# Eight query projections around an attention of eight head couples: two of them placed whole, or three of them in halves, on one Trainium2 core

## The chip, the cores and the metric

The kernel runs on one core of a Trainium2 chip (trn2). Five instruction streams are written out by hand and meet at semaphores: TensorE (PE in the profile, its weight loads PEld), VectorE (DVE), ScalarE (ACT), GpSimd (POOL) and SyncE (SP), which issues nearly all of the transfers. The metric is the device time of one execution in microseconds.

## The reference

A two-layer network on 256 tokens of 1024 features. Layer one is a short convolution mixer and a gated feed-forward block. Layer two is an attention block followed by a second feed-forward block. Cut to the part in question:

```python
kv = nsa_shared_kv(rmsnorm(x, kv_norm), w_kv, cmp_pe, cmp_w1, cmp_b1, cmp_w2)
qg = h @ w_qg                          # h is [256, 1024]: 16 heads x 64 of queries, 48 gate columns
# per head: compressed, selected and windowed branch
o_c = softmax(q @ k_cmp + bias_c) @ v_cmp       # 15 compressed blocks
o_s = softmax(q @ k_slc + bias_s) @ v_slc       # 256 keys, causal
o_w = softmax(q @ k_win + bias_w) @ v_win       # 256 keys, causal
o = g[..., 0:1] * o_c + g[..., 1:2] * o_s + g[..., 2:3] * o_w
x = x + o @ w_o
```

`k_cmp` and `v_cmp` come from a small gelu network over blocks of 32 tokens: `gelu(blk @ cmp_w1 + cmp_b1) @ cmp_w2`.

## The kernel before

**Pieces.** All large weights come in pieces of 128x1024 f32 (512 KB). A float32 product is made of three matmuls on two fp32r parts of each operand, so each piece is treated three times before TensorE uses it: SP loads it into `staged`, ScalarE casts it into `w_hi` (function `lead`, L529), and VectorE subtracts the two and writes the remainder to `w_lo` (function `rest`, L746). Six such remainders are given to GpSimd instead (L438). Pieces rotate through six slots; the load of a piece waits for the remainder of the piece six places earlier, the cast of a piece for TensorE's use of that earlier piece. The counters `hi_up`, `lo_up` and `used_up` rise by one for each piece in order, so one engine's remainders and another's must follow each other in piece order.

**Order.** `B_ORDER` lists the pieces of the attention block: 12 for keys and values, four `w1` (the first product of the compressing network), the gate, eight `q` (one for each couple of heads, a 128x128x8 product of 24 matmuls of 256 columns, L1090 to L1092), and eight of the output projection (`o`). TensorE, VectorE and ScalarE walk this list up to `("q", Q_BEFORE - 1)`, here `("q", 4)`. At each entry `b` ScalarE casts piece b + 6 and VectorE makes its remainder, so that the walk covers the pieces up to the third `o` piece.

**Compressed keys and values.** When all four `w1` products are in, VectorE computes a tanh gelu (L938 to L961, then L964 and L966 behind a ScalarE tanh, L684); TensorE's `compressed()` (L1266, L1269) waits for it (`hidden_done`) and stands behind `q` 3; VectorE copies its result out (L972, L975).

**Attention.** Heads go in couples: `scores(i)` (L1344 to L1350), then per head an exponential on ScalarE (L696), `weigh` on VectorE (L1023 to L1034, the far spans) and GpSimd (L486, the near spans), `turn` on TensorE (transposes, L1362 to L1373), copies out of PSUM (`keep_turned`, L1043 and L1045 on VectorE, L708 on ScalarE) and `attend` (L1387 to L1394). VectorE's `bias_and_maximum` (L991, L994, L1013) is what the next but one couple's exponentials wait for. On TensorE couple `i` is the stretch `turn(2i)`, `turn(2i + 1)`, `scores(i + 2)`, `attend(i)`. `q` 5 stands between `scores(0)` and `scores(1)`; `q` 6 and `q` 7 stand whole between the two turns of couples 0 and 5 (`Q_CYCLE = {0: 6, 5: 7}`). After couple 5 the output projection (`project`) is woven into the last two couples.

**What follows a query.** Each query product is copied out by VectorE (`query`, L912), and `scores(i)` waits for the copy of query max(i, 2). Queries 3 to 7 share one PSUM bank.

Of the kernel before, what the change touches and what calls it, by code (L numbers as in the profile page):

```python
# [50 lines left out]
for _name, _n in (("gains", 6 * KT), ("a_taps", 3 * AU), ("f_taps", 2 * 2 * FU * 3), ("pe", 2 * 16),  # L51
# [5 lines left out]


B_ORDER = ([("cmp", t) for t in range(4)] + [("key", t) for t in range(4)] + [("val", t) for t in range(4)]
           + [("w1", 0), ("gate", 0), ("w1", 1), ("q", 0), ("w1", 2), ("q", 1), ("w1", 3)] + [("q", t) for t in range(2, 8)]  # L60
           + [("o", t) for t in range(8)])
NB = len(B_ORDER)
UP_SLOTS, DOWN_SLOTS = 6, 3
# [2 lines left out]
KEEP_WARM = 5  # L66
O_FIRST = B_ORDER.index(("o", 0))

Q_BEFORE = 5
Q_RING = 6  # L70


# [1 line left out]
def q_index(t):  # L74
    return B_ORDER.index(("q", t))
# [50 lines left out]
def build(nc, xT, xt, par, final, hot, rel, a_up, a_down, f_up, f_down, b_up, b_down, scratch, out):  # L126
    piece = plan_pieces()
    ctx = ExitStack()
    with ctx:
# [284 lines left out]
        @block.gpsimd  # L414
        def _(pool):
            nc.gpsimd.memset(ones[:], 1.0).then_inc(consts_done, 1)
            nc.gpsimd.memset(ident[:], 0.0).then_inc(consts_done, 1)
            nc.gpsimd.memset(eps[:], EPS).then_inc(consts_done, 1)
            nc.gpsimd.memset(rowmask[:], 1.0).then_inc(consts_done, 1)
            pool.wait_ge(consts_done, 4)  # L420
            nc.gpsimd.affine_select(out=ident[:], in_=ident[:], compare_op=ALU.not_equal, fill=1.0, base=0,
                                    pattern=[[-1, P]], channel_multiplier=1).then_inc(consts_done, 1)


            nc.gpsimd.affine_select(out=rowmask[:], in_=rowmask[:], compare_op=ALU.is_ge, fill=0.0, base=P - CL,
                                    pattern=[[0, 1]], channel_multiplier=-1).then_inc(consts_done, 1)
            nc.gpsimd.memset(vc[:], 0.0).then_inc(consts_done, 1)

            def pads(n):
                nc.gpsimd.memset(shifted[:, :, :, 0:2], 0.0).then_inc(padded, 1)  # L430

            def rest(st, kind, k, c):

                q = piece_of(st, kind, k, c)
                hi, lo = (hi_up, lo_up) if kind == "up" else (hi_down, lo_down)
                pool.wait_ge(hi, q["n"] + 1)
                pool.wait_ge(lo, q["n"])
                nc.gpsimd.tensor_tensor(w_lo[:, q["slot"], :], staged[:, min(q["slot"], UP_SLOTS), :],  # L438
                                        w_hi[:, q["slot"], :].bitcast(F32), ALU.subtract).then_inc(lo, 1)

            pads(0)


            pool.wait_ge(rows_copied, 1)
            pool.dma_start(scratch, rows_sb).then_inc(rows_stored, 16)
            pool.wait_ge(rows_stored, 16)
            diagonals = bass.AP(tensor=scratch.tensor, offset=0, ap=[[1, P], [384, HEADS], [1, T]])
            pool.dma_start(bias[:], diagonals).then_inc(bias_landed, 16)
            nc.gpsimd.memset(ends_bias[:], NEG).then_inc(ends_ready, 1)
            pool.wait_ge(ends_ready, 1)  # L450
            pool.wait_ge(bias_landed, 16)
            nc.gpsimd.tensor_copy(ends_bias[:, :, 0, 0:NC0], bias[:, :, P + CL - 1::CS]).then_inc(ends_ready, 1)
            nc.gpsimd.tensor_copy(ends_bias[:, :, 1, :], bias[:, :, CL - 1::CS]).then_inc(ends_ready, 1)
            rest("a", "down", AU - 1, 0)
            rest("f0", "up", 1, 1)
            rest("f0", "down", FU - 1, 0)
            rest("b", "up", 3, 0)
            for j in range(2):

                pool.wait_ge(tokens_shifted, j + 1)  # L460
                if j:

                    pool.wait_ge(block_lo_done, 1)
                tok, pe_j = tokens[:, j, 0, 0:1], params[:, PAR["pe"] + 16 * j:PAR["pe"] + 16 * j + 16]
                tok = bass.AP(tensor=tok.tensor, offset=tok.offset, ap=[tok.ap[0], [2, 16], [T, GROUPS], [CS, NC]])
                pe_j = pe_j.unsqueeze(2).unsqueeze(3).to_broadcast([P, 16, GROUPS, NC])
                nc.gpsimd.tensor_tensor(block_in.rearrange("p (i g c) -> p i g c", i=16, g=GROUPS), tok, pe_j,
                                        ALU.add).then_inc(block_done, 1)
                pool.wait_ge(block_hi_done, j + 1)
                nc.gpsimd.tensor_tensor(blocks[j][:, 1, :], block_in, blocks[j][:, 0, :].bitcast(F32),  # L470
                                        ALU.subtract).then_inc(block_lo_done, 1)

            pool.wait_ge(block_lo_done, 2)
            for r in range(2):
                nc.gpsimd.memset(ends_soft[:, r, :, :, NC:32], 0.0).then_inc(zeroed, 1)
            def lower_ends(i):

                pool.wait_ge(ends_maxed, i + 1)
                nc.gpsimd.tensor_tensor(ends_of(i), ends_of(i), over_ends(ends_max[:, i % 2]), ALU.subtract).then_inc(ends_lowered, 1)

            lower_ends(0)
            for e in range(HEADS):

                pool.wait_ge(weighted, e + 1)
                for n in NEAR:
                    q = nc.gpsimd.tensor_scalar(span(e, n), span(e, n), stats_of(e, 12 + n, 13 + n), None, ALU.mult)  # L486
                q.then_inc(normed, 1)
                if e % 2:
                    nc.gpsimd.tensor_tensor(ends_of(e // 2), ends_of(e // 2), over_ends(stats[:, e // 2 % 2, :, 12:14]),
                                            ALU.mult).then_inc(ends_weighted, 1)  # L490
                elif e + 2 < HEADS:
                    lower_ends(e // 2 + 1)

            pool.wait_ge(headed, HEADS // 2)
            pads(1)
            rest("f1", "up", 1, 1)
            rest("f1", "down", FU - 1, 0)
# [236 lines left out]
        def _(dve):  # L734
# [180 lines left out]
            for b, (what, t) in enumerate(B_ORDER):  # L915
# [50 lines left out]
                    nc.vector.tensor_tensor(hid, th, z, ALU.mult).then_inc(hidden_done, 1)  # L966
                if what == "q":
                    query(t)
                if (what, t) == ("q", 3):
                    dve.wait_ge(cmp_mm, 1)  # L970
                    for p in range(2):
                        nc.vector.tensor_copy(keysT[HD * p:HD * p + HD, :, 0:NC],  # L972
                                              bank[6][0:HD, 128:128 + 60].rearrange("p (a q c) -> p a q c", a=2, q=2)[:, :, p, :])
                    for p in range(2):
                        q = nc.vector.tensor_copy(vc[32 * p:32 * p + NC, :, HD * p:HD * p + HD],  # L975
                                                  bank[6][32 * p:32 * p + NC, 256:512].rearrange("p (a q c) -> p a q c", a=2, q=2)[:, :, p, :])
                    q.then_inc(cmp_done, 1)
                rest("b", "up", b + AHEAD, 0)
                if (what, t) == ("q", Q_BEFORE - 1):
                    break  # L980
            dve.wait_ge(bias_landed, 16)
            dve.wait_ge(ends_ready, 3)
            dve.wait_ge(zeroed, 2)
# [70 lines left out]

            bias_and_maximum(0)
            bias_and_maximum(1)
            query(5)
            for i in range(HEADS // 2 - 1):
                weigh(2 * i)
                bias_and_maximum(2 * i + 2)  # L1060
                weigh(2 * i + 1)
                keep_turned(2 * i)
                bias_and_maximum(2 * i + 3)
                if i >= 1:
                    rest_heads(i - 1)
                if i in Q_CYCLE:
                    query(Q_CYCLE[i])
                keep_turned(2 * i + 1)
            weigh(HEADS - 2)
            rest("b", "up", q_index(5) + AHEAD, 0)  # L1070
# [16 lines left out]
        def _(pe):  # L1087
# [164 lines left out]
            def queries(t):  # L1252
                if t == 3:

                    pe.wait_ge(gate_done, 1)
                elif t > 3:

                    pe.wait_ge(b_evacuated, 8 + t)
                product(piece_of("b", "up", q_index(t), 0), q_bank(t), gq_hi, gq_lo, True)

            def compressed():

                pe.wait_ge(hidden_done, 1)
# [12 lines left out]
            for b in range(4, q_index(Q_BEFORE - 1) + 1):  # L1276
# [9 lines left out]
                if what == "q":  # L1286
# [4 lines left out]
                    if t == 0:  # L1291
# [3 lines left out]
                            mm = nc.tensor.transpose(bank[7][:, T + 3 * HEADS * k:T + 3 * HEADS * (k + 1)],  # L1295
                                                     gateT[:, k * P:k * P + P], ident[0:3 * HEADS, 0:3 * HEADS])
                        mm.then_inc(gate_turned, 1)
                    if t == 3:
                        compressed()
                    continue  # L1300
                pe.wait_ge(lo_up, q["n"] + 1)
# [105 lines left out]
            pe.wait_ge(cmp_done, 1)  # L1407
            pe.wait_ge(vals_done, 2)
            scores(0)
            queries(5)  # L1410
            scores(1)
            for i in range(HEADS // 2 - 2):
                turn(2 * i)
                if i in Q_CYCLE:
                    queries(Q_CYCLE[i])
                turn(2 * i + 1)
                scores(i + 2)
                attend(i)
# [15 lines left out]


SPANS = [None, None, (0, P), (P, T), (P + T, P), (2 * P + T, T)]
Q_CYCLE = {0: 6, 5: 7}
LEAD_AFTER = {3: 5, 5: 6, 11: 7}
NEAR, FAR = (2, 4), (3, 5)


def head_of(e):
# [10 lines left out]
NOTHING = ([], [], [])  # L1453


AFTER_POOL = {("f0", "down", 0, 0), ("f0", "up", 2, 0), ("b", "up", 4, 0), ("f1", "down", 0, 0), ("f1", "up", 2, 0)}


def UPS(st, k, i=0):
# [73 lines left out]
```

## Time and profile before

| | before |
|---|---|
| median of 3 runs | 632.47 us (631.91 to 633.13) |
| the profiled execution, whole | 633.22 us |
| span in the profile | 631.5 us |
| granted TensorE clock, mean | 0.994 |
| PE / PEld busy | 97% / 85% |
| DVE / ACT / POOL busy | 77% / 62% / 9% |
| projections of the attention block | about 295 to 355 us |
| attention of eight couples | about 355 to 423 us |

The profiled execution spends 633.22 - 631.5 = 1.7 us outside the span. A timeline row gives the start, the time from start to end of a run of like instructions, the engine, line, operation and shapes, and in square brackets how long the engine sat idle before it and what released it. Matmuls overlap, so the time that one takes of TensorE is the distance from its start to the start of the next, not its own duration. The same holds by some 0.1 us for VectorE and ScalarE.

### The profile page before, as it was taken

The numbers are of one execution on the slowest core, as the hardware profiler recorded it, in microseconds if no ns is written. First come the engines' busy times: TensorE is split into PE (matmuls) and PEld (weight loads), VectorE is DVE, ScalarE is ACT, GpSimd is POOL, SyncE is SP. The second block draws the span as 40 slices with busy tenths as digits, with TensorE's granted clock in tenths as the row PEclk, the third lists the DMA queues.
The fourth block names the chain that finished last, engine by engine and source line by source line (L and its number), as shares of the span: only waits on it lengthen the run. The fifth ranks groups of instructions, "written<-read, shape, count | busy, mean of one in ns | idle before, by whom it ended". The sixth has DMA issues, their size and how long they took to land.

```text
span 631.5 us, 11277 instructions
## 1 busy us (share of the span) xinstructions
PE 610.9 (97%) x3738; PEld 534.1 (85%) x3738; DVE 485.1 (77%) x939; ACT 388.6 (62%) x708; POOL 59.4 (9%) x78
## 2 busy tenths in 40 slices
PE   7999999999999999999999898998999999999995
PEld 7999997888888888888989776777888888888884
DVE  4787756788888777777878789847788888777865
ACT  6644445666666666668556478717766666666644
POOL 0110002000000000011131144421000000000010
PEclk8999999999999999999999999999999999999998
DMA  8797432465656555761476400033365555555531
GB/s 310 290 336 241 179 133 100 166 203 194 205 201 202 199 189 179 287 241 34 146 245 214 142 2 2 1 101 133 118 206 193 209 201 207 192 178 195 199 101 66
DMA packets 30640, 109.55 MB, mean 173 GB/s; under 512 B 3419, under 2 KB 3691, under 8 KB 30476
## 3 DMA queue, kind: packets, MB, share of 16 engines
q1 hardware_dynamic: 30044, 106.97, 48.6%
q0 software_dynamic: 560, 2.12, 0.9%
q8 instruction: 20, 0.33, 0.2%
q14 instruction: 16, 0.13, 0.1%
HBM read 108.00 MB, written 1.07 MB: 173 GB/s over the span
## 4 chain that ended last, share of the span: by engine, by line
PE 88%; DVE 5%; ACT 3%; issue 2%; POOL 1%; DMA 1%; SPq 0%; DVEq 0%; ACTq 0%
PE bank L1129 24%; PE bank L1090 15%; PE bank L1091 15%; PE bank L1092 15%; PE bank L1133 13%; POOL work L486 1%; PE bank L1109 1%; DVE work L1013 1%; PE bank L1362 1%; DMA staged<-in_a_up 1%; ACT work L533 1%; PE bank L1320 1%; PE bank L1150 1%; PE bank L1110 1%; ACT w_hi L529 1%
## 5 line engine op out<-in xcount | busy, mean ns | idle before, releaser
L746 DVE TENSOR_TENSOR w_lo<-staged,w_hi 128x1024 fp32r<-128x1024 f32 x191 | 236.6, 1247 | 41.9 <-ACT w_hi L529 41.9
L529 ACT ACTIVATE w_hi<-staged 128x1024 fp32r<-128x1024 f32 x197 | 199.8, 1046 | 26.6 <-PE bank L1092 15.7
L1129 PE MATMUL bank<-gx,w_hi 128*128 128x512 f32 x672 | 167.2, 391 | 0.0
L1129 PEld LDWEIGHTS bank<-gx,w_hi 128*128 128x128 f32 x672 | 123.2, 188 | 23.8
L1133 PEld LDWEIGHTS bank<-gx,w_lo 128*128 128x128 f32 x672 | 91.7, 190 | 6.6
L1133 PE MATMUL bank<-gx,w_lo 128*128 128x256 f32 x672 | 93.7, 282 | 0.0
L1090 PE MATMUL bank<-w_hi,y 128*128 128x512 f32 x208 | 81.5, 392 | 0.0
L1091 PE MATMUL bank<-w_lo,y 128*128 128x512 f32 x208 | 81.5, 392 | 0.0
L1092 PE MATMUL bank<-w_hi,y 128*128 128x512 f32 x208 | 80.9, 389 | 0.0
L615 ACT ACTIVATE work<-work,params 128x256 f32<-128x256 f32 x96 | 44.2, 504 | 57.4 <-DVE work L847 39.2
L1090 PE MATMUL bank<-gx,w_hi 128*128 128x256 f32 x256 | 73.4, 287 | 2.6 <-DVE w_lo L746 2.1
L1091 PE MATMUL bank<-gx,w_hi 128*128 128x256 f32 x256 | 73.1, 285 | 0.0
L1092 PE MATMUL bank<-gx,w_lo 128*128 128x256 f32 x256 | 73.0, 285 | 0.0
L629 ACT ACTIVATE y<-work 128x256 fp32r<-128x256 f32 x52 | 21.7, 418 | 77.8 <-DVE work L868 59.8
L438 POOL TENSOR_TENSOR w_lo<-staged,w_hi 128x1024 fp32r<-128x1024 f32 x6 | 14.5, 2415 | 424.9 <-ACT w_hi L529 424.9
L1090 PEld LDWEIGHTS bank<-gx,w_hi 128*128 128x128 f32 x256 | 49.8, 195 | 3.8 <-DVE w_lo L746 3.0
L1091 PEld LDWEIGHTS bank<-gx,w_hi 128*128 128x128 f32 x256 | 49.8, 194 | 0.2
L1092 PEld LDWEIGHTS bank<-gx,w_lo 128*128 128x128 f32 x256 | 49.8, 194 | 0.0
L847 DVE TENSOR_TENSOR work<-bank,work 128x512 f32<-128x512 f32 x44 | 30.4, 691 | 24.6 <-ACT work L611 24.5
L1092 PEld LDWEIGHTS bank<-w_hi,y 128*128 128x128 f32 x208 | 39.1, 188 | 8.5
L1090 PEld LDWEIGHTS bank<-w_hi,y 128*128 128x128 f32 x208 | 39.2, 189 | 7.1
L854 DVE SCALAR_TENSOR_TENSOR work<-work,params 128x256 f32<-128x256 f32 x96 | 42.4, 479 | 3.6 <-ACT work L615 3.5
(160 smaller groups left out, 818.7 us busy)
## 6 DMA issues: line engine op xcount, KB each, us to landing
staged<-in_f_up SPq DMA_DIRECT2D x88, 512.0 KB, 5.2
staged<-in_f_down SPq DMA_DIRECT2D x44, 512.0 KB, 3.3
staged<-in_a_up SPq DMA_DIRECT2D x24, 512.0 KB, 7.3
staged<-in_b_up SPq DMA_DIRECT2D x24, 512.0 KB, 4.3
staged<-in_a_down SPq DMA_DIRECT2D x8, 512.0 KB, 3.5
staged<-in_b_down SPq DMA_DIRECT2D x8, 512.0 KB, 4.2
bias<-bias_rows POOLq DMA_DIRECT2D x1, 2048.0 KB, 11.5
bias<-in_xT SPq DMA_DIRECT2D x4, 256.0 KB, 5.2
```

Source lines behind the costliest of these rows:

```text
L438: nc.gpsimd.tensor_tensor(w_lo[:, q["slot"], :], staged[:, min(q["slot"], UP_SLOTS), :], w_hi[:, q["slot"], :].bitcast(F32), ALU.subtract) ...
L529: nc.scalar.activation(w_hi[:, q["slot"], 0:n], staged[:, s, 0:n], ACT.Copy).then_inc(hi, 1)
L615: nc.scalar.activation(conv[:, r, c, :], shifted[:, r, c, 2:2 + T], ACT.Copy, scale=tap(st, c, i, k, 2)).then_inc(tapped[st], 1)
L629: nc.scalar.activation(y_hi[:, r * T:(r + 1) * T], conv[:, r, 1, :], ACT.Copy).then_inc(y_hi_done[st], 1)
L746: nc.vector.tensor_tensor(w_lo[:, q["slot"], 0:n], staged[:, s, 0:n], w_hi[:, q["slot"], 0:n].bitcast(F32), ALU.subtract).then_inc(lo, 1)
L847: nc.vector.tensor_tensor(shifted[:, r, :, 2:2 + T], pair_of(st, k, 0), shifted[:, r, :, 2:2 + T], ALU.add).then_inc(scaled[st], 1)
L854: nc.vector.scalar_tensor_tensor(conv[:, r, c, :], shifted[:, r, c, 1:1 + T], tap(st, c, i, k, 1), conv[:, r, c, :], ALU.mult, ALU.add).th ...
L1090: nc.tensor.matmul(out_ap, whi, xhi, start=start, stop=False, skip_group_check=True)
L1091: nc.tensor.matmul(out_ap, whi, xlo, start=False, stop=False, skip_group_check=True)
L1092: return nc.tensor.matmul(out_ap, wlo, xhi, start=False, stop=stop, skip_group_check=True)
L1129: nc.tensor.matmul(dst, w_hi[:, s, kt * P:kt * P + P], gx[:, kt, :], start=kt == 0, stop=False, skip_group_check=True)
L1133: mm = nc.tensor.matmul(dst[:, 0:T], w_lo[:, s, kt * P:kt * P + P], gx_hi[:, kt, :], start=False, stop=kt == KT - 1, skip_group_check=True)
```

## The change

Query 4 leaves the walk ahead of attention and takes the place of query 5 between the first two scores. Queries 5, 6 and 7 are cut into two halves of 12 matmuls each, and the six halves stand one in each of couples 0 to 5, between the two turns. To let `compressed()` come one query earlier, the last `w1` piece is put ahead of `q` 1, and `compressed()` stands behind `q` 2. The walk on ScalarE and VectorE ends one entry earlier, and VectorE's walk no longer makes the remainders of the second and third `o` piece: GpSimd makes them in half tiles behind heads 5, 7, 9 and 11. ScalarE's casts of the later `o` pieces stand behind heads 1, 3, 7 and 11 (before: 3, 5 and 11).

```diff
-           + [("w1", 0), ("gate", 0), ("w1", 1), ("q", 0), ("w1", 2), ("q", 1), ("w1", 3)] + [("q", t) for t in range(2, 8)]
+           + [("w1", 0), ("gate", 0), ("w1", 1), ("q", 0), ("w1", 2), ("w1", 3), ("q", 1)] + [("q", t) for t in range(2, 8)]
...
-Q_BEFORE = 5
+Q_BEFORE = 4
...
+            def rest_half(b, h):
+
+                q = piece_of("b", "up", b, 0)
+                cols = slice(h * 512, h * 512 + 512)
+                if h == 0:
+                    pool.wait_ge(hi_up, q["n"] + 1)
+                    pool.wait_ge(lo_up, q["n"])
+                r = nc.gpsimd.tensor_tensor(w_lo[:, q["slot"], cols], staged[:, q["slot"], cols],
+                                            w_hi[:, q["slot"], cols].bitcast(F32), ALU.subtract)
+                if h:
+                    r.then_inc(lo_up, 1)
...
                 elif e + 2 < HEADS:
                     lower_ends(e // 2 + 1)
+                if e in REST_AFTER:
+                    rest_half(*REST_AFTER[e])
...
-                if (what, t) == ("q", 3):
+                if (what, t) == ("q", 2):
                     dve.wait_ge(cmp_mm, 1)
...
-                rest("b", "up", b + AHEAD, 0)
                 if (what, t) == ("q", Q_BEFORE - 1):
                     break
+                rest("b", "up", b + AHEAD, 0)
...
-            query(5)
+            query(4)
...
-                if i in Q_CYCLE:
-                    query(Q_CYCLE[i])
+                if i % 2 and i < 6:
+                    query(Q_HALVES + i // 2)
                 keep_turned(2 * i + 1)
...
+            def half_queries(t, n):
+
+                q = piece_of("b", "up", q_index(t), 0)
+                s = q["slot"]
+                if n == 0:
+                    pe.wait_ge(b_evacuated, 8 + t)
+                    pe.wait_ge(lo_up, q["n"] + 1)
+                for kt in range(4 * n, 4 * n + 4):
+                    mm = three(q_bank(t), w_hi[:, s, kt * P:kt * P + P], w_lo[:, s, kt * P:kt * P + P], gq_hi[:, kt, :], gq_lo[:, kt, :],
+                               kt == 0, kt == KT - 1)
+                if n:
+                    mm.then_inc(used_up, 1)
...
-                    if t == 3:
+                    if t == 2:
                         compressed()
...
-            queries(5)
+            queries(4)
             scores(1)
             for i in range(HEADS // 2 - 2):
                 turn(2 * i)
-                if i in Q_CYCLE:
-                    queries(Q_CYCLE[i])
+                half_queries(Q_HALVES + i // 2, i % 2)
                 turn(2 * i + 1)
...
-Q_CYCLE = {0: 6, 5: 7}
-LEAD_AFTER = {3: 5, 5: 6, 11: 7}
+Q_HALVES = 5
+LEAD_AFTER = {1: 4, 3: 5, 7: 6, 11: 7}
 NEAR, FAR = (2, 4), (3, 5)
+REST_AFTER = {5: (q_index(Q_BEFORE - 1) + AHEAD, 0), 7: (q_index(Q_BEFORE - 1) + AHEAD, 1),
+              9: (q_index(Q_BEFORE) + AHEAD, 0), 11: (q_index(Q_BEFORE) + AHEAD, 1)}
```

In addition the fourth `o` piece's remainder on VectorE waits for the count that GpSimd's last half gives (`AFTER_POOL`).

## Rows read from the trace of the kernel before

**Rows 1.** The page's busy times by engine, over the whole span.
```profile
PE 610.9 (97%) x3738; PEld 534.1 (85%) x3738; DVE 485.1 (77%) x939; ACT 388.6 (62%) x708; POOL 59.4 (9%) x78
```

**Rows 2.** TensorE's waits, 338 to 412 us: in total, times, longest.
```profile
PE bank L1362 <- POOL work L486: 6.3, 6, 1.4
PE bank L1344 <- DVE stats L1013: 0.5, 1, 0.5
```

**Rows 3.** Windows: length, then busy time per engine, granted clock, DMA share, GB/s.
```profile
371.30:377.80 6.50, 5.51 (x49) 3.90 (x48) 6.16 (x34) 6.04 (x21) 3.29 (x6) 1.00 0.00 1
397.40:405.60 8.20, 8.20 (x74) 6.81 (x73) 6.62 (x35) 6.17 (x21) 3.30 (x6) 1.00 0.01 2
```

**Rows 4.** Timeline of TensorE, couple 0, which holds query 6.
```profile
363.13 0.66 PE L1362 MATMUL bank<-ident,work 128*128 128x128 f32 x4 [1.37 <-POOL work L486]
...
363.76 0.36 PE L1090 MATMUL bank<-gq_hi,w_hi 128*128 128x256 f32 x1
363.96 0.28 PE L1091 MATMUL bank<-gq_lo,w_hi 128*128 128x256 f32 x1
...
366.71 0.60 PE L1362 MATMUL bank<-ident,work 128*128 128x128 f32 x4
...
367.68 0.51 PE L1344 MATMUL bank<-work 64*128 64x143 f32 x4
```

**Rows 5.** Timeline of TensorE, couple 1, which holds no query, and the next turn.
```profile
371.31 0.66 PE L1362 MATMUL bank<-ident,work 128*128 128x128 f32 x4
...
373.18 0.66 PE L1362 MATMUL bank<-ident,work 128*128 128x128 f32 x4 [0.99 <-POOL work L486]
...
374.20 0.52 PE L1344 MATMUL bank<-work 64*128 64x143 f32 x4
...
377.83 0.66 PE L1362 MATMUL bank<-ident,work 128*128 128x128 f32 x4
```

**Rows 6.** Timeline of VectorE, one couple from copy to copy, and the copy of query 7.
```profile
374.31 0.42 DVE L1043 COPY work<-bank 128x256 f32<-128x256 f32 x1
...
377.99 0.17 DVE L1030 TENSOR_TENSOR stats<-stats,gate 128x6 f32<-128x6 f32 x1
...
380.29 0.41 DVE L1051 TENSOR_TENSOR gx<-bank,gx 128x256 fp32r<-128x256 f32 x1
380.83 0.42 DVE L1043 COPY work<-bank 128x256 f32<-128x256 f32 x1
...
381.96 0.17 DVE L1030 TENSOR_TENSOR stats<-stats,gate 128x6 f32<-128x6 f32 x1
...
401.18 0.42 DVE L912 TENSOR_SCALAR work<-bank 128x256 f32<-128x256 f32 x1 [0.92 <-PE bank L1092]
```

**Rows 7.** Timeline of GpSimd, head 1 in couple 0, then the couple of rows 6.
```profile
365.60 0.29 POOL L489 TENSOR_TENSOR work<-work,stats 128x60 f32<-128x60 f32 x1
...
378.26 1.39 POOL L486 TENSOR_SCALAR work<-work,stats 128x128 f32<-128x128 f32 x2 [0.91 <-DVE stats L1030]
379.62 0.29 POOL L489 TENSOR_TENSOR work<-work,stats 128x60 f32<-128x60 f32 x1
382.23 1.39 POOL L486 TENSOR_SCALAR work<-work,stats 128x128 f32<-128x128 f32 x2 [2.32 <-DVE stats L1030]
```

**Rows 8.** Timeline of TensorE from the compressed product to the second scores.
```profile
351.26 0.33 PE L1266 MATMUL bank<-work,params 128*64 128x60 f32 x2
...
351.85 0.39 PE L1090 MATMUL bank<-gq_hi,w_hi 128*128 128x256 f32 x1
...
354.90 0.52 PE L1344 MATMUL bank<-work 64*128 64x143 f32 x4
...
356.46 0.38 PE L1090 MATMUL bank<-gq_hi,w_hi 128*128 128x256 f32 x1
...
360.13 0.52 PE L1344 MATMUL bank<-work 64*128 64x143 f32 x4 [0.54 <-DVE stats L1013]
```

**Rows 9.** Timeline of VectorE at the start of attention.
```profile
356.16 1.23 DVE L746 TENSOR_TENSOR w_lo<-staged,w_hi 128x1024 fp32r<-128x1024 f32 x1 [0.72 <-ACT w_hi L529]
357.30 0.21 DVE L991 TENSOR_TENSOR work<-bank,ends_bias 128x60 f32<-128x60 f32 x1
...
359.90 0.42 DVE L912 TENSOR_SCALAR work<-bank 128x256 f32<-128x256 f32 x1
```

**Rows 10.** Timeline of VectorE ahead of the compressed product.
```profile
344.38 0.42 DVE L912 TENSOR_SCALAR work<-bank 128x256 f32<-128x256 f32 x1
344.97 1.23 DVE L746 TENSOR_TENSOR w_lo<-staged,w_hi 128x1024 fp32r<-128x1024 f32 x1 [0.17 <-ACT w_hi L529]
...
348.84 0.29 DVE L966 TENSOR_TENSOR work<-work 128x120 f32<-128x120 f32 x1
```

**Rows 11.** GpSimd's whole remainder (line view: ns min/median/max), and two-input work of GpSimd and VectorE together.
```profile
L438 POOL TENSOR_TENSOR w_lo<-staged,w_hi x6: 2384/2408/2483, 93.4 to 614.0; 128x1024 fp32r<-128x1024 f32 x6
...
332.61 2.39 POOL L470 TENSOR_TENSOR gx<-work,gx 128x960 fp32r<-128x960 f32 x1 [8.53 <-ACT gx L674]
...
333.51 2.57 DVE L746 TENSOR_TENSOR w_lo<-staged,w_hi 128x1024 fp32r<-128x1024 f32 x1 [0.62 <-ACT w_hi L529]
```

**Rows 12.** The page's group of ScalarE's casts: busy, mean ns; idle before.
```profile
L529 ACT ACTIVATE w_hi<-staged 128x1024 fp32r<-128x1024 f32 x197 | 199.8, 1046 | 26.6 <-PE bank L1092 15.7
```

More of the change, by code:

```diff
@@ L1453 @@
 NOTHING = ([], [], [])
-AFTER_POOL = {("f0", "down", 0, 0), ("f0", "up", 2, 0), ("b", "up", 4, 0), ("f1", "down", 0, 0), ("f1", "up", 2, 0)}
+AFTER_POOL = {("b", "up", q_index(Q_BEFORE + 1) + AHEAD, 0), ("f0", "down", 0, 0), ("f0", "up", 2, 0), ("b", "up", 4, 0), ("f1", "down", 0, 0), ("f1", "up", 2, 0)}
 def UPS(st, k, i=0):
```

## The prediction

> **What bounds the kernel now.** I read the page first: TensorE is busy 97% of the span, VectorE 77% [rows 1]. TensorE's work is the same before and after, matmul for matmul, so the change can only win time in which TensorE stands still, and it can lose only where it makes new standstill. The second view is therefore the list of TensorE's waits over the stretch that the change touches: 6 waits for GpSimd's L486, 6.3 us in all, and one of 0.5 us for VectorE's L1013 [rows 2]. The third view, the windows by couple, shows the pattern: a couple without a query lasts 6.5 us with TensorE busy for 5.5, a couple with a whole query 8.2 us with TensorE never idle; the granted clock is 1.00 in both, the upper of its two levels (2.4 GHz) [rows 3]. Last the timelines, for the chain that sets the 6.5 us.
>
> That chain is a cycle. Let K be the start of VectorE's copy of the odd head's turn, 374.31. Its L1030 is at K + 3.7, GpSimd's L486 starts at K + 3.95 and is through at 379.62 = K + 5.3, the next odd turn starts 0.1 later, takes about 1 us, and the next copy is at 380.83 = K + 6.52 [rows 6, 7]. VectorE is itself nearly full: its last step L1051 starts at 380.29 and gives way about 0.34 later, at K + 6.3 [rows 6]. TensorE, for its part, goes from one even turn to the next in 6.52 us, from 371.31 to 377.83, and waits 0.99 of it [rows 5]; with query 6 it takes 371.31 - 363.13 = 8.18 [rows 4, 5]. The query costs 366.71 - 363.76 = 2.95 us of TensorE [rows 4] but lengthens the couple by only 1.66: a couple has room for 1.29 us of other work. Couples 0 and 5 hold 2.95 each and use the room up; couples 1 to 4 leave it empty.
>
> **Step 1: query 4 leaves the stretch ahead of attention.** The stretch from `compressed()` to the first scores is 354.90 - 351.26 = 3.64 [rows 8] and keeps its make-up. What moves is the whole of it, one query earlier. A query there is worth 2.96 (from 351.85 to 354.90 less 0.09 of signal) [rows 8]. TensorE would be at `compressed()` at 351.26 - 2.96 = 348.30. But `compressed()` needs VectorE's L966, and that is not one query earlier. Before, it ends at 348.84 + 0.29 = 349.13, 2.1 us ahead of its use [rows 8, 10]. Between 343 and 349 VectorE has its queue full: the same remainders, the copy of query 1 and the gelu in another order, with one gap, from the end of L912's share (344.38 + 0.33) to 344.97, 0.26 us [rows 10]. The earlier `w1` piece lets only that gap go. So L966 ends at about 348.87, with the signal 349.0, and TensorE stands still for 0.7 us. A new wait; it eats a quarter of this step. The first scores start 351.26 - 349.0 = 2.26 earlier, at 352.64.
>
> **Step 2: one remainder less in front of the first maximum.** Before, the first scores are out at about 356.5 but VectorE makes the third `o` piece's remainder until 357.30, and only then starts L991 [rows 8, 9]. Without L746 it starts 0.1 to 0.15 after the scores, 1.71 after their start, at 354.35: 2.95 earlier than 357.30. The second scores wait for L1013 as before (359.90 to 360.13 [rows 8, 9]); query 4 in the place of query 5 ends at 352.64 + 1.56 + 2.98 = 357.2, L1013 at 356.95 with the signal 357.2, so that this wait of 0.5 us goes, but turn 0 hangs on VectorE, ScalarE and GpSimd, not on the scores. It comes 2.95 earlier, at 360.18 instead of 363.13 [rows 4]. **Gain of steps 1 and 2: 2.95 us.**
>
> **Step 3: halves in six couples.** In the whole query the first matmul takes 363.96 - 363.76 = 0.20 and the other 23 take 2.75 / 23 = 0.12 each [rows 4]. A half is 0.20 + 11 x 0.12 = 1.52. A couple in which TensorE never waits then takes 8.18 - 2.95 + 1.52 = 6.75. Is the cycle quick enough? TensorE comes to the next odd turn 0.97 (turn, 366.71 to 367.68 [rows 4]) + 3.63 (scores and attend, 374.20 to 377.83 [rows 5]) + 0.63 (even turn, 363.13 to 363.76 [rows 4]) + 1.52 = 6.75 after the last, which is K + 5.67; GpSimd is through at K + 5.3, plus 0.1. It holds by 0.28. In couple 0 the pipeline is not yet in step: GpSimd releases turn 1 at 365.60 = 2.47 after turn 0 [rows 4, 7], with the signal 2.55, TensorE is there after 0.63 + 1.52 = 2.15. That leaves 0.40, and 0.05 for a turn that starts cold: 7.20. Six couples took 2 x 8.18 + 4 x 6.52 = 42.44 and take 7.20 + 5 x 6.75 = 40.95. **Gain 1.49 us.** The seventh couple has the same chain at its odd turn and stays.
>
> **Step 4: copies of queries 5 to 7.** They lie on VectorE in couples 1, 3 and 5, between L1051 and the next copy. VectorE reaches that place at K + 6.32, the copy adds 0.34, and 6.66 is still below 6.75. But `scores(7)` waits for the copy of query 7: written at K + 6.32 + 0.42 = 6.74 [rows 6], signalled at 6.81, wanted at 6.75 - 0.11 = 6.64. **Loss 0.15 us.** The copies of 5 and 6 are wanted two couples later and cost nothing.
>
> **Step 5: half tiles on GpSimd.** A whole remainder is 2.41 us there [rows 11], 60 columns are 0.29 [rows 7]; on the line through both 512 columns are 1.3 (bounds: half of 2.41, 1.2, and 1.6 if it is crowded as VectorE's is in rows 11 by a third). Behind an odd head GpSimd is free from 379.62 + 0.29 = 379.91 to 382.23 [rows 7], 2.3 us. The half ends at 381.2. The first VectorE instruction after it that reads two SBUF operands is L1030 at 381.96 [rows 6]; until then VectorE works on PSUM operands. So the cover is 0.75 us towards VectorE and 1.0 towards L486: cost nothing. If the cover were gone, VectorE would stand as in rows 11, where L746 takes 2.57 instead of 1.23 beside a GpSimd L470 that began 0.9 earlier. That row speaks against the change in general.
>
> The Trainium skill says why, in "SBUF — State Buffer", section "Who interferes with whom": a VectorE instruction with two SBUF inputs and a GpSimd one that reads SBUF exclude each other for a whole instruction, the first to issue wins. The trace agrees with the 2.57. Applied to the place of the halves the rule gives the same zero; should they slip by 0.75 it gives the slower rival below.
>
> **Step 6: casts.** ScalarE's four casts (1.05 each [rows 12]) stand behind odd heads, where it waits for attend's end anyway. They wait for TensorE's use of queries 4 to 7, which in each case lies ahead of the turn that the cast stands behind. The `o` pieces are first wanted after couple 6. Nothing, and at most 0.3 each if an exponential is held up. The load of the last `o` piece hangs on GpSimd's second half and comes some 30 us later than before, still 20 us ahead of need; the second layer's feed-forward loads hang on VectorE's remainders behind head 14, which keep their distance from the end of attention.
>
> **Sum:** 2.95 + 1.49 - 0.15 = 4.29 us. Against the profiled execution: span 631.5 - 4.3 = 627.2, whole 633.22 - 4.29 = 628.9. That execution was 0.75 above the median; from the median 632.47 it is 628.2.
>
> **Rivals.** *More is gained:* VectorE reaches L966 in time, the wait of step 1 is small. For it: VectorE's order is new and a copy may wait less. Against it: from 343.25 to 349.13 only 0.26 us are free. Without the wait 627.5. *The handovers cost more, because VectorE sets the odd couples:* 6.66 against 6.75 leaves no room; if each of couples 1, 3 and 5 takes VectorE's 6.66 plus the 0.2 us by which its queue stood empty before the copy at 380.83 [rows 6], if the even couples don't win it back, and if the halves cost 1.6 instead of 1.52, then 3 x 0.11 + 6 x 0.08 and a wait of `compressed()` longer by half a remainder (0.6) give 628.2 + 1.4 = 629.6. *It does not do what it says:* the couples keep their standstill and the half comes on top, 6.52 + 1.52 = 8.04 in each of six couples, 48.2 instead of 42.4; with step 1 and 2 that is 632.47 - 2.95 + 5.8 = 635.3. This decides if the odd head's chain started only behind the half. The code has no such wait, and couple 0 shows a query filling 1.29 of standstill. *Slower by the shared port:* the half is still running when L1030 and the far spans' L1034 want SBUF, or holds up L486. Point from which it decides: a half later or longer by 0.75. Price by rows 11: 2.57 - 1.23 = 1.35 on VectorE's part of the cycle, four times 5.4, less the 0.3 of slack in one couple, and as much again, 1.1, for L486 pushed behind it: 628.2 + 6.2 = 634.4. *No difference:* parts of both last cases in one or two couples, or a later stage that gives the time back; I see none, since everything after couple 6 hangs on the attention itself.
>
> **How the numbers follow.** A measurement of this kernel tells 0.2%, 1.3 us, from no change. Forecast 0.66 (its own range 627.4 to 629.2), more gained 0.10, handovers 0.13, no difference 0.06, the two slower ones 0.05 together. The range takes in the first three with the spread of three runs, 0.6: 626.8 to 630.3. Faster by over 0.2% (below 631.2): 0.89; within: 0.07; slower: 0.04.
>
> **What would show it.** TensorE's waits: L1362 for L486 down to about two or three (turn 0, turn 1, turn 13), the 0.5 for L1013 gone, a new one of 0.7 on L1266 for L966. First scores at 352.6, turn 0 at 360.2, even turns 6.75 apart, turn 12 at 401.1 (before 405.58). GpSimd has four remainders of 128x512 of 1.2 to 1.3 us each, and VectorE's L1030 keeps its 0.17 behind them. The prediction is wrong if a couple takes over 7 us, if L966 ends before 348.3, or if turn 13 and later stand still more than before.

## The result

The changed kernel takes 628.51 us (median of 4 runs, 627.70 to 628.83) against 632.25 us for the kernel before: ratio 0.9928, 95% interval 0.9915 to 0.9941, so 0.7% faster (the two medians by themselves give 628.51 / 632.25 = 0.9941). The forecast was 628.2 in a range of 626.8 to 630.3. Two later rounds of the same kernel gave 0.9923 (0.9906 to 0.9939) and 0.9943 (0.9926 to 0.9960). In the last of them four of six runs had a low granted clock, which the forecast knew nothing of; that is taken up below.

The page of the changed kernel, its busy times:

```profile
span 627.1 us, 11282 instructions
PE 610.6 (97%) x3738; PEld 534.4 (85%) x3738; DVE 482.8 (77%) x937; ACT 388.2 (62%) x708; POOL 63.3 (10%) x82
```

TensorE's busy time is within 0.3 us of that in [rows 1], the span is 4.4 us shorter. TensorE's waits between 338 and 412 us (total, times, longest), which answer to [rows 2]:

```profile
PE bank L1389 <- POOL work L498: 2.5, 3, 1.4
PE bank L1293 <- DVE work L980: 0.4, 1, 0.4
```

The six waits for GpSimd (6.3 us) are three (2.5), the 0.5 for L1013 is gone, and a new one stands in front of the compressed product. The timeline of TensorE from that product to the first turn, which answers to [rows 8] and the first of [rows 4]:

```profile
348.99 0.33 PE L1293 MATMUL bank<-work,params 128*64 128x60 f32 x2 [0.45 <-DVE work L980]
...
352.64 0.51 PE L1371 MATMUL bank<-work 64*128 64x143 f32 x4
...
357.25 0.52 PE L1371 MATMUL bank<-work 64*128 64x143 f32 x4
...
360.25 0.66 PE L1389 MATMUL bank<-ident,work 128*128 128x128 f32 x4 [1.37 <-POOL work L498]
```

And the same view for couples 1, 5 and 6, where [rows 5] stood:

```profile
367.46 0.66 PE L1389 MATMUL bank<-ident,work 128*128 128x128 f32 x4
...
369.60 0.60 PE L1389 MATMUL bank<-ident,work 128*128 128x128 f32 x4
...
374.20 0.66 PE L1389 MATMUL bank<-ident,work 128*128 128x128 f32 x4
...
394.44 0.66 PE L1389 MATMUL bank<-ident,work 128*128 128x128 f32 x4
...
396.59 0.60 PE L1389 MATMUL bank<-ident,work 128*128 128x128 f32 x4
...
397.69 0.52 PE L1371 MATMUL bank<-work 64*128 64x143 f32 x4
...
401.33 0.66 PE L1389 MATMUL bank<-ident,work 128*128 128x128 f32 x4
...
403.06 0.66 PE L1389 MATMUL bank<-ident,work 128*128 128x128 f32 x4 [0.86 <-POOL work L498]
```

Couple 1 takes 374.20 - 367.46 = 6.74 and TensorE goes into its odd turn without a wait. To compare executions that don't begin equally fast I use one anchor, the gate's transposes ahead of the third w1 piece (338.62 before, 338.70 after), and one end, the first projection matmul (408.29 before, 403.90 after). The four rows, first of the kernel before, then of the changed kernel:

```profile
338.62 0.32 PE L1295 MATMUL bank<-ident,work 48*128 48x48 f32 x2
...
408.29 0.48 PE L1090 MATMUL bank<-w_hi,gx 128*128 128x512 f32 x1
```

```profile
338.70 0.32 PE L1322 MATMUL bank<-ident,work 48*128 48x48 f32 x2
...
403.90 0.47 PE L1104 MATMUL bank<-w_hi,gx 128*128 128x512 f32 x1
```

That stretch is 69.67 before and 65.20 after: **4.47 us less**. Behind it both kernels take the same, 631.5 - 408.29 = 223.2 and 627.1 - 403.90 = 223.2. Everything gained is gained in this stretch and nothing of it is given back later.

### The profile page after: what moved, and what is told of

The parts are those of the page before. It is cut to its first block, busy times and chain, and to the rows that moved or that the text cites. A ratio compares the mean times of both kernels' runs of the same rounds, so it can differ in the third digit from the quotient of the medians.

```text
span 627.1 us, 11282 instructions
## 1 busy us (share of the span) xinstructions
PE 610.6 (97%) x3738; PEld 534.4 (85%) x3738; DVE 482.8 (77%) x937; ACT 388.2 (62%) x708; POOL 63.3 (10%) x82
## 4 chain that ended last, share of the span: by engine, by line
PE 88%; DVE 5%; ACT 3%; issue 1%; DMA 1%; POOL 0%; SPq 0%; DVEq 0%; ACTq 0%
PE bank L1143 24%; PE bank L1104 14%; PE bank L1105 14%; PE bank L1106 14%; PE bank L1147 13%; DVE w_lo L760 2%; PE bank L1123 1%; PE bank L1389 1%; ACT w_hi L543 1%; DMA staged<-in_a_up 1%; ACT work L547 1%; PE bank L1421 1%; PE bank L1164 1%; PE bank L1414 1%; PE bank L1124 1%
```

## The experiments

The first theory is the prediction's: the couple has room for a half but not for a whole query, and VectorE's queue sets the start of the compressed product. Rivals are that only the earlier start counts, that VectorE and GpSimd hold each other up and so take the gain, and that the remainders on GpSimd bring most of it.

### The changed kernel again

> The changed kernel itself, as the mark for its neighbours on the same chip. Expected: ratio to the kernel before 0.993, span 627.1 us, turn 12 some 41.1 us after turn 0.

Ratio 0.9923, span 627.8, 41.1 us from turn 0 to turn 12. But the compressed product stands 11.41 us behind the anchor instead of 10.29. The windows (length, then busy time and count of PE, PEld, DVE, ACT, POOL, granted clock, DMA share, GB/s) of this execution:

```profile
338.00:342.00 4.00, 4.00 (x36) 3.81 (x35) 3.96 (x7) 2.62 (x3) 0.00 (x0) 0.99 0.57 198
342.00:346.00 4.00, 4.00 (x23) 4.00 (x23) 3.79 (x10) 1.06 (x1) 0.00 (x0) 0.58 0.86 295
```

and of the execution profiled first:

```profile
342.00:346.00 4.00, 4.00 (x36) 4.00 (x36) 3.79 (x11) 1.38 (x3) 0.00 (x0) 1.00 0.87 267
```

In the one, TensorE's clock goes down to 0.50 (the lower level, 1.2 GHz) from 341.9 to 345.3 us; in the other it does not. This was not in my reckoning, and it is taken up again below. For the other experiments I therefore compare pieces of the timeline that lie clear of it.

### Halves without the earlier start

```diff
-                if i in Q_CYCLE:
-                    queries(Q_CYCLE[i])
+                if i < 4:
+                    half_queries(6 + i // 2, i % 2)
```

(in the kernel before; VectorE copies them out in couples 1 and 3)

> Query 4 stays ahead of attention, query 5 between the first two scores; only queries 6 and 7 are cut into halves, in couples 0 to 3. My theory (a couple has 1.29 us of standstill which a half of 1.52 fills): couples of 7.2, 6.75, 6.75, 6.75, 6.52, 6.52 us, 40.5 against 42.4 before, so 1.95 us faster than the kernel before, ratio 0.997. Rival (the half comes on top of the 6.52): four couples of 8.04, no gain, 45.2, ratio 1.004.

Ratio 0.9975 (0.9962 to 0.9987). The even turns of couples 3 to 5:

```profile
384.02 0.66 PE L1375 MATMUL bank<-ident,work 128*128 128x128 f32 x4
...
390.77 0.66 PE L1375 MATMUL bank<-ident,work 128*128 128x128 f32 x4
392.63 0.66 PE L1375 MATMUL bank<-ident,work 128*128 128x128 f32 x4 [0.99 <-POOL work L486]
...
397.29 0.66 PE L1375 MATMUL bank<-ident,work 128*128 128x128 f32 x4
```

Couple 3, with a half, takes 6.75; couple 4, without, 6.52 and its 0.99 of waiting. From anchor to first projection 67.73, against 69.67 before: 1.94 less where 1.95 was expected. The rival, a half on top of the 6.52, is out.

### Whole queries in three couples

```diff
-                half_queries(Q_HALVES + i // 2, i % 2)
+                if i % 2 == 0:
+                    queries(Q_HALVES + i // 2)
```

(VectorE copies them out in the same even couples)

> The changed kernel with queries 5, 6 and 7 whole in couples 0, 2 and 4 instead of in halves in couples 0 to 5. My theory: three couples of 8.18 and three of 6.52, 44.1 us from turn 0 to turn 12 against 41.1 with halves, so 3.0 us slower than the changed kernel (ratio to before about 0.998). Rival (the gain of the change lies in the earlier start alone and the halves do nothing): same as the changed kernel, 0.993.

Ratio 0.9983 (0.9970 to 0.9996). Turn 0 and turn 12:

```profile
361.54 0.66 PE L1389 MATMUL bank<-ident,work 128*128 128x128 f32 x4 [1.37 <-POOL work L498]
...
405.65 0.66 PE L1389 MATMUL bank<-ident,work 128*128 128x128 f32 x4
```

The couples take 8.18, 6.53, 8.18, 6.52, 8.18, 6.52, in all 44.11 us from turn 0 to turn 12 against 401.33 - 360.25 = 41.08 with halves: 3.03 more, 3.0 expected. Against the 405.58 - 363.13 = 42.45 of the kernel before, the loop with three whole queries is 1.7 us longer and eats more than half of the earlier start; with halves it is 1.4 shorter.

### The last w1 piece in its old place

```diff
-           + [... ("w1", 2), ("w1", 3), ("q", 1)] ...
+           + [... ("w1", 2), ("q", 1), ("w1", 3)] ...
```

> The changed kernel with the last w1 piece behind query 1 again; compressed() stays behind query 2. My theory (VectorE's queue, not the w1 product, sets the time of L980, and the order frees only one gap of 0.26 us): the compressed product starts 0.26 us later, the whole 0.3 us slower than the changed kernel. Rival (the product itself has to be early): the w1 product ends one query later, 2.9 us, and the compressed product with it, 2 to 3 us slower.

Ratio 0.9943 (0.9921 to 0.9964), five runs. The compressed product:

```profile
349.31 0.33 PE L1293 MATMUL bank<-work,params 128*64 128x60 f32 x2 [0.73 <-DVE work L980]
```

That is 349.31 - 338.74 = 10.57 behind the anchor, 0.28 more than with the piece moved (0.26 expected). The rival's 2 to 3 us are out. Moving the w1 product is worth a quarter of a microsecond, since VectorE's queue decides. That is little against what the neighbourhood of the two products goes with in other executions: the 1.1 us of `after_again`.

### The halves behind the even heads

```diff
-REST_AFTER = {5: ..., 7: ..., 9: ..., 11: ...}
+REST_AFTER = {4: ..., 6: ..., 8: ..., 10: ...}
```

> The changed kernel with the same four halves behind the even heads 4, 6, 8 and 10, where GpSimd is free for only 0.9 us. If VectorE's L1044 and GpSimd's half exclude each other for a whole instruction: VectorE's L1044 of the odd head stands 0.6 us, L498 starts 0.8 us late, of which 0.28 is slack: 0.5 us for each of four couples, 2 us slower than the changed kernel. If only GpSimd's own queue counts: L498 0.36 us late, 0.1 us for each, 0.4 us slower.

Ratio 0.9969 (0.9957 to 0.9981). GpSimd and VectorE in couple 3:

```profile
383.11 1.27 POOL L488 TENSOR_TENSOR w_lo<-staged,w_hi 128x512 fp32r<-128x512 f32 x1
384.50 1.39 POOL L498 TENSOR_SCALAR work<-work,stats 128x128 f32<-128x128 f32 x2
```

```profile
383.57 0.18 DVE L1041 RECIPROCAL stats<-stats 128x6 f32<-128x6 f32 x1
383.79 0.61 DVE L1044 TENSOR_TENSOR stats<-stats,gate 128x6 f32<-128x6 f32 x1
384.43 0.73 DVE L1048 TENSOR_SCALAR work<-work,stats 128x256 f32<-128x256 f32 x2
```

L1044, six columns from two SBUF operands, takes 0.61 instead of 0.17 and ends at 384.40, when the half ends (384.38). L1041, with one SBUF operand, ran at its usual speed beside the same half. The same 0.61 stands in all four couples that hold a half. So these two instructions exclude each other. The price is 1.2 us where I expected 2: the couples from 2 to 5 take 6.97, 6.97, 7.09 and 7.32, which is 0.23, 0.23, 0.33 and 0.43 over those of the changed kernel. L1044 met the half late and lost 0.44, not 0.6. Less the 0.28 of slack that L498 has, 0.16 a couple would be left; why the later couples lose more than the earlier ones is not worked out. The expectation was wrong in size; that L1044 stands until the half is through is shown.

### Whole remainders on GpSimd

```diff
-                if e in REST_AFTER:
-                    rest_half(*REST_AFTER[e])
+                if e in (7, 11):
+                    rest("b", "up", q_index(Q_BEFORE - 1 + (e == 11)) + AHEAD, 0)
```

> The changed kernel with the two remainders on GpSimd whole, behind heads 7 and 11, instead of in halves behind 5, 7, 9 and 11. My theory: a whole one runs 2.4 us from 383.0, ends 0.1 us after VectorE's L1044 wants to start and before L498 does, so each costs 0.1 to 0.2 us at VectorE and next to nothing at TensorE: within 0.3 us of the changed kernel. Rival (the port costs as L746 beside L470 did, 1.35 us each): 2.0 to 2.7 us slower.

Ratio 0.9938 (0.9920 to 0.9955).

```profile
382.97 2.37 POOL L438 TENSOR_TENSOR w_lo<-staged,w_hi 128x1024 fp32r<-128x1024 f32 x1
385.56 1.39 POOL L498 TENSOR_SCALAR work<-work,stats 128x128 f32<-128x128 f32 x2 [0.22 <-DVE stats L1044]
```

The whole piece ends at 385.34, and L1044 of the next head takes its usual 0.17 from 385.29, so the 0.1 to 0.2 us that I expected it to lose are not there. From anchor to first projection 65.22 against 65.20. Dividing the remainders into halves gains nothing here; a whole one just fits the same gap. The halves only leave a wider margin.

### The remainders on VectorE

```diff
+                rest("b", "up", b + AHEAD, 0)
                 if (what, t) == ("q", Q_BEFORE - 1):
                     break
-                rest("b", "up", b + AHEAD, 0)
```

(and the other one ahead of the fourth `o` piece's, behind head 14; none on GpSimd)

> The changed kernel with the two remainders back on VectorE, one at the end of the walk, ahead of the first maximum, one behind head 14's weights; GpSimd makes none in attention. My theory: the first remainder has to wait for its cast and ends at 355.0, the first maximum (354.4 in the changed kernel) starts 0.55 us later, and so does all behind it; the second costs nothing: 0.5 us slower. Rival (the remainders were worth a whole L746 each): 2.4 us slower.

Ratio 0.9950 (0.9935 to 0.9965).

```profile
356.98 1.23 DVE L758 TENSOR_TENSOR w_lo<-staged,w_hi 128x1024 fp32r<-128x1024 f32 x1 [0.72 <-ACT w_hi L541]
358.13 0.21 DVE L1003 TENSOR_TENSOR work<-bank,ends_bias 128x60 f32<-128x60 f32 x1
```

```profile
355.73 0.51 PE L1370 MATMUL bank<-work 64*128 64x143 f32 x4
...
363.95 0.66 PE L1388 MATMUL bank<-ident,work 128*128 128x128 f32 x4 [1.38 <-POOL work L498]
```

The first scores start at 355.73 and turn 0 at 363.95, 8.22 later, against 360.25 - 352.64 = 7.61 in the changed kernel: 0.61 lost (0.55 expected). So the whole move to GpSimd is worth 0.6 us, not two remainders of 1.2.

### The gelu ahead of a remainder

```diff
+                if (what, t) == ("q", 2):
+                    rest("b", "up", b - 1 + AHEAD, 0)
                 if what == "q":
                     query(t)
...
-                rest("b", "up", b + AHEAD, 0)
+                if (what, t) != ("q", 1):
+                    rest("b", "up", b + AHEAD, 0)
```

> The changed kernel with one remainder (L760, the second last of the walk) made behind the gelu's last two steps instead of ahead of them. My theory (TensorE's 0.45 us wait on L1293 is VectorE's queue): L980 ends 1.1 us earlier, the wait goes, the compressed product starts about 348.4 instead of 349.0 and all behind it is 0.6 us earlier; 0.1% faster than the changed kernel, ratio to before 0.992. Rival (the first maximum hangs on something else): wait gone, but turn 0 where it was, no gain.

Ratio 0.9936 (0.9921 to 0.9951). In its profiled execution the clock fell at 342 again, and the compressed product started without a wait, 350.20 - 338.91 = 11.29 behind the anchor. But in `after_again`, where the clock fell too, it also started without a wait:

```profile
349.77 0.33 PE L1293 MATMUL bank<-work,params 128*64 128x60 f32 x2
```

So this trace does not show that the edit removes the wait, nor the 0.6; where the clock falls, the edit is worth the 0.1 us between 11.41 and 11.29. The next run settles it.

### The same, and the copy of query 7 earlier

```diff
+                if i == 5:
+                    query(7)
                 if i >= 1:
                     rest_heads(i - 1)
-                if i % 2 and i < 6:
+                if i in (1, 3):
                     query(Q_HALVES + i // 2)
```

> The changed kernel with the gelu's last two steps ahead of the second last remainder, and with VectorE's copy of query 7 ahead of that couple's head remainder (L1065). If my step 4 (scores(7) waits 0.15 us for the copy and that is lost) holds: couple 5 takes 6.74 instead of 6.88 and turn 12 to the first projection stays 2.57 us, 0.15 won. Rival (the profile of the changed kernel shows turn 13 standing 0.13 less than before): couple 5 6.74, turn 13 waits 0.13 more, nothing won. With the gelu ahead, and no fall of the clock: span 625.4; with one at 342 us, some 1 to 2 us more.

Ratio 0.9924 (0.9908 to 0.9940). No fall at 342 in the profiled execution:

```profile
348.40 0.33 PE L1298 MATMUL bank<-work,params 128*64 128x60 f32 x2
```

348.40 - 338.63 = 9.77 instead of 10.29: 0.52 won by making one remainder later. For the copy of query 7, couples 5 and 6:

```profile
393.86 0.66 PE L1394 MATMUL bank<-ident,work 128*128 128x128 f32 x4
...
396.98 0.52 PE L1376 MATMUL bank<-work 64*128 64x143 f32 x4
...
400.62 0.66 PE L1394 MATMUL bank<-ident,work 128*128 128x128 f32 x4
...
402.47 0.66 PE L1394 MATMUL bank<-ident,work 128*128 128x128 f32 x4 [0.98 <-POOL work L498]
```

Couple 5 takes 6.76 instead of 401.33 - 394.44 = 6.89, but turn 13 comes 1.85 behind turn 12 instead of 1.73. In sum, from anchor to first projection, 64.69 against 65.20: 0.51 less, all of it the gelu's. What `scores(7)` loses, turn 13 gives back, because its release hangs on VectorE and GpSimd and not on TensorE. The rival holds.

### The w1 products apart again, and together in the kernel before

```diff
-           + [... ("w1", 2), ("w1", 3), ("q", 1)] ...
+           + [... ("w1", 2), ("q", 1), ("w1", 3)] ...
...
+                if (what, t) == ("q", 2):
+                    rest("b", "up", b - 1 + AHEAD, 0)
                 if what == "q":
                     query(t)
...
-                rest("b", "up", b + AHEAD, 0)
+                if (what, t) != ("w1", 3):
+                    rest("b", "up", b + AHEAD, 0)
```

> The same gelu order, but the last w1 piece again behind query 1, so that the two w1 products of narrow matmuls (120 and 60 columns) do not stand together. L980 then ends about 348.5 and the compressed product starts 0.2 us later than without the swap back. Theory (the falls of the granted clock to 0.50 at 342 to 345 us, seen in five of seven profiles with the two products together and in none of three with a query between, come from the 3.6 us of narrow matmuls): no fall at 342 here, mean clock 0.995 to 0.998 in all runs, spans 625.6 to 627. Rival (the falls come by chance or from the earlier attention): as many low clocks (0.99 to 0.993) as in the kernels before.

Ratio 0.9921 (0.9908 to 0.9934), 627.54 us (627.19 to 628.47), the lowest median of all kernels, though its interval overlaps those of its neighbours. The compressed product:

```profile
347.81 0.33 PE L1296 MATMUL bank<-work,params 128*64 128x60 f32 x2
```

That is 347.81 - 337.93 = 9.88 behind the anchor. No fall at 342 in the profile, and mean clocks of 0.996 to 0.998 in all five runs. By itself this does not decide, since `gelu_first_copy7`, with the two products together, had only one low run of six.

The other direction, a single edit in the kernel before:

```diff
-           + [... ("w1", 2), ("q", 1), ("w1", 3)] ...
+           + [... ("w1", 2), ("w1", 3), ("q", 1)] ...
```

> The kernel before with nothing changed but the last w1 piece put ahead of query 1 (the compressed product stays behind query 3). The work and all waits on the path are the same, so without the clock: same as the kernel before, ratio 1.000. If the two w1 products together bring the clock down: a fall to 0.50 at about 342 us in the profile or in some of the runs, 1.5 to 3 us longer in those. If the fall needs the earlier attention: none.

633.25 us (631.87 to 636.37), ratio 1.0015 (1.0001 to 1.0028). Its profiled execution shows no fall and the same stretches as the kernel before (69.69 from anchor to projection). But of its 12 runs five have a mean clock of 0.990 to 0.993 and spans of 632.7 to 634.6; the runs of the kernel before, 50 in those three comparisons, have 0.994 to 0.998 and none has a span over 632.0. So long executions with a low clock come with this one edit alone, without the earlier attention. No trace shows where in them the clock fell.

### A third round of the changed kernel

> The changed kernel once more, to count falls of the clock in it: until now one of its 8 executions had a mean clock of 0.993, while the kernel before with the swapped w1 piece alone had 5 of 12 at 0.993 or less and the kernel before none of 50. If the two w1 products together bring the fall with them in every kernel alike: one to three of the runs at 0.993 or less, with spans near 627.8, the others at 626.0 to 627.1. If the changed kernel is spared: none.

629.86 us (627.83 to 630.64), ratio 0.9943. Four of six runs at 0.992 or 0.993 with spans of 628.1 to 628.9, two at 0.998 with 626.1 and 626.2. The profile is one of the four:

```profile
338.00:342.00 4.00, 4.00 (x37) 3.81 (x35) 3.96 (x6) 2.88 (x3) 0.00 (x0) 1.00 0.63 210
342.00:346.00 4.00, 4.00 (x22) 4.00 (x22) 3.79 (x11) 1.09 (x2) 0.00 (x0) 0.57 0.87 264
```

## Why the prediction was right, and where it was not

The sum was 4.29 us; the stretch lost 4.47 and the span 4.4.

**Steps 1 and 2, 2.95.** From the anchor, turn 0 came at 363.13 - 338.62 = 24.51 and comes at 360.25 - 338.70 = 21.55: 2.96. The new wait for the gelu, put at 0.7, shows as 0.45 of idle and a start at 348.99, where 349.0 was said; `gelu_first_copy7`, without it, gets 0.52 back. It and `w1_old_order` show that VectorE's queue makes the wait. The first scores come 2.34 earlier from the anchor (2.26 said), which leaves 0.62 for step 2; `rests_on_vector` confirms that from its other end (0.61).

**Step 3, 1.49.** Turn 0 to turn 12 was 42.45 and is 41.08, and 0.13 of the 41.08 belongs to step 4: a gain of 1.50. Couple 0 takes 7.21 (7.20 said), the next four 6.74 to 6.76 (6.75), couple 5 6.89. `halves_only` and `whole_queries` show it apart from the rest.

**Step 4, a loss of 0.15.** This term failed. The delay of `scores(7)` is there (397.69 - 396.59 = 1.10 instead of 0.97), but the step forgot that turn 13, one couple on, stands waiting anyway: its wait went from 0.99 to 0.86. In the kernel before, turn 12 and turn 13:

```profile
405.58 0.66 PE L1362 MATMUL bank<-ident,work 128*128 128x128 f32 x4
...
407.44 0.65 PE L1362 MATMUL bank<-ident,work 128*128 128x128 f32 x4 [0.99 <-POOL work L486]
```

The net loss is nil, and `gelu_first_copy7` shows it. 4.29 + 0.15 = 4.44 is what the trace has.

**Step 5, nothing.** The four halves take 1.27 or 1.28 us (1.3 said) and lie where they should. In couple 3:

```profile
382.98 1.28 POOL L488 TENSOR_TENSOR w_lo<-staged,w_hi 128x512 fp32r<-128x512 f32 x1
```

It ends 1.03 us before L1044 starts at 385.29 (0.75 said). `halves_even` shows that the danger was real, but also that the rival's price for it, 1.35 us a time from [rows 11], was three times what L1044 lost. `whole_tiles` shows that even a whole remainder fits. **Step 6, nothing:** the last 223.2 us are the same.

**What I did not price.** I read the granted clock, 1.00 in the rows of the stretch, and took it as given. The change puts two products of narrow matmuls (120 and 60 columns) next to each other, from 338.9 to 342.5 us. In six of the ten profiles with that order the clock falls to 0.50 shortly before the second of them is through, between 341.8 and 342.7 us. In the trace of `after_again` TensorE would have been at the compressed product 10.29 - 0.45 = 9.84 behind the anchor and is there at 11.41: the lower clock costs it 1.6 us. The wait for the gelu, 0.45, takes up part of that, and 11.41 - 10.29 = 1.1 us are lost. The final time still lay in the range in all three rounds (medians of 628.1, 628.5 and 629.9), but that is in part luck: with four of six runs low, the third came within half a microsecond of the upper bound, by a term that the sum does not have.

That the neighbourhood of the two products brings the falls rests on counts. With the two together (the changed kernel, its variants, and the kernel before with that edit) 27 of 66 runs have a mean clock of 0.993 or less; with a query between them (`halves_only`, `w1_old_order`, `gelu_first_old_w1`) 1 of 16, and of 61 runs of the kernel before, in four comparisons, none. These sums flatter the case, since 17 of the 27 come from two rounds in which no variant with a query between ran; in the two rounds that had both kinds it is 10 of 32 against 1 of 16. The strongest evidence is `before_new_w1`, one edit and 5 of 12 against 0 of 17 in the same round. A mean clock does not say where the clock fell, either. Of the 14 profiles 11, those of both kernels among them, have another fall, 3.4 us long, between 9 and 16 us,

```profile
10.00:14.00 4.00, 3.88 (x20) 3.88 (x21) 3.45 (x7) 3.28 (x5) 0.00 (x0) 0.57 1.05 405
```

(the kernel before) where `before_new_w1` has 1.00 and reaches the anchor at 337.40 instead of 338.62. But all six profiles with a fall at 341 to 349 us have the two products together, and the four with a query between them have none. Not shown is that TensorE's narrow matmuls are the cause and not something else that the swap moves, for it also changes the order on ScalarE and VectorE. Not settled are why only some executions fall, why `halves_even` has seven low runs of ten, and the one low run of `w1_old_order`, which has no trace.

The Trainium skill, in "TensorE: Matmul & The Clock Gate", Part 1, describes a gate with these two levels that goes by how busy TensorE has been. The levels agree with the rows. Of idle time ahead of these falls the rows show nothing: PE busy 4.00 of 4.00.

## What to carry to other kernels

Where TensorE waits a little in every round of a loop, independent matmuls cut to about the size of that wait are worth more than whole ones in a few rounds: find the loop's cycle without TensorE, subtract, and cut to fit. After moving work earlier, look for what in another engine's queue does not move with it; here one remainder made later wins a further 0.5 us. And look at the granted clock in several executions, not in one, before you put narrow products side by side.

## What was not expected of the hardware

TensorE's granted clock fell from 1.00 to 0.50 in the middle of the kernel, with TensorE busy in the records throughout: for 3.4 us in `after_again` and `after_third`, and for 6.8 us in `halves_even`,

```profile
342.00:348.00 6.00, 6.00 (x29) 6.00 (x30) 4.75 (x11) 1.06 (x2) 0.00 (x0) 0.50 0.80 258
```

where the compressed product came 12.81 us behind the anchor instead of 10.29. Expected in kind, but worth seeing in so small an operation: one of VectorE on six columns with two SBUF operands stood for 0.44 us beside a GpSimd subtraction, while one with a single SBUF operand did not.
